# Projections of a group's last head placed 9, 14 and 9 pieces past the unit's last, where it was 5

## What is computed

```
for i in range(2):
    h = rmsnorm(x, pre_norm[i])
    proj = h @ w_in                     # 1024 x 3088 (GLA), 1024 x 5152 (SSD)
    # GLA: q, k, v, gate r, low-rank decay;  SSD: z, (x, B, C) through a conv of 4 taps, dt
    y = chunked_scan(proj) * silu(gate) # four heads or groups, a state carried from chunk to chunk
    y = rmsnorm_per_head(y) @ w_out
    x = x + rmsnorm(y, post_norm[i])
```

## Time and profile before

| | |
|---|---|
| median of 3 runs | 1531.34 us (1528.44 to 1532.91) |
| profiled execution | 1527.04 us |
| its span, first to last instruction | 1525.3 us |
| PE busy | 1422.1 us (93%) |
| DVE busy | 1170.3 us (77%) |
| ACT busy | 837.6 us (55%) |
| POOL busy | 241.8 us (16%) |
| mean granted TensorE clock | 0.982 of full |

### The profile page before, as it was taken

One profiled execution on the slowest core, in us unless ns is written; L12 is line 12 of the kernel. 1 busy time (PEld: TensorE's weight loads), 2 busy tenths in 40 slices (PEclk: granted clock), 3 DMA queues, 4 the chain that ended last, 5 costly groups with the idle time before them and its releaser, 6 DMA issues. The chain is left out here.

```text
span 1525.3 us, 31313 instructions
## 1 busy us (share of the span) xinstructions
PE 1422.1 (93%) x11554; PEld 1181.4 (77%) x11554; DVE 1170.3 (77%) x2592; ACT 837.6 (55%) x1877; POOL 241.8 (16%) x421
## 2 busy tenths in 40 slices
PE   6999998799999969999999999989999999999985
PEld 5989887667888759898888988867777777777754
DVE  4566687767777987968886998976879787687775
ACT  4745555365656545546565754654666474655451
POOL 5010122011422100011120220220012110000012
PEclk9999999999999989999999999999999999999998
DMA  7474556255576343458844855742675665555541
GB/s 201 129 222 127 184 174 219 79 170 166 156 200 191 105 129 96 139 125 222 250 119 134 275 149 157 226 128 78 195 226 150 179 180 151 173 153 156 174 139 62
DMA packets 284162, 247.34 MB, mean 162 GB/s; under 512 B 32696, under 2 KB 250908, under 8 KB 283340
## 3 DMA queue, kind: packets, MB, share of 16 engines
q1 hardware_dynamic: 274348, 212.51, 47.0%
q0 software_dynamic: 9664, 32.84, 7.9%
HBM read 184.59 MB, written 65.00 MB: 164 GB/s over the span
## 5 line engine op out<-in xcount | busy, mean ns | idle before, releaser
L1452 PE MATMUL bank<-h,w 128*128 128x268 f32 (+1 forms) x4752 | 834.7, 330 | 23.1 <-ACT w L863 16.2
L1452 PEld LDWEIGHTS bank<-h,w 128*128 128x128 f32 x4752 | 701.0, 191 | 100.9 <-issue 24.7
L879 DVE TENSOR_TENSOR w<-w_raw,w 128x1024 fp32r<-128x1024 f32 x132 | 160.9, 1219 | 38.0 <-ACT w L863 37.6
L848 PE MATMUL bank<-s_w_out,s_yt_hi 128*128 128x512 f32 (+2 forms) x544 | 169.8, 402 | 3.8 <-DVE s_ys L2546 3.8
L863 ACT ACTIVATE w<-w_raw 128x1024 fp32r<-128x1024 f32 x132 | 138.7, 1051 | 7.9 <-DMA w_raw<-in_ssd_w_in_dram 7.7
L1530 DVE SCALAR_TENSOR_TENSOR conv<-before_conv,cw,conv 128x260 f32<-128x260 f32 (+2 forms) x216 | 125.3, 580 | 4.2
L848 PEld LDWEIGHTS bank<-s_w_out,s_yt_hi 128*128 128x128 f32 (+2 forms) x544 | 97.0, 182 | 30.8 <-issue 4.4
L848 PE MATMUL bank<-g_w_out,g_ot_hi 128*128 128x512 f32 (+2 forms) x288 | 97.5, 427 | 1.5 <-DVE g_ot_lo L2088 1.3
L848 PE MATMUL bank<-s_w_out,s_yt_lo 128*128 128x512 f32 x240 | 95.6, 398 | 0.0
L2630 ACT ACTIVATE s_yt_hi<-bank 128x512 fp32r<-128x512 f32 (+1 forms) x36 | 20.1, 558 | 124.7 <-PE bank L2621 124.6
L2333 ACT ACTIVATE s_decay<-s_decay,t_ac 128x128 f32<-128x128 f32 (+1 forms) x288 | 85.5, 379 | 1.2
(11 more groups left out here) (258 smaller groups left out, 2465.5 us busy)
## 6 DMA issues: line engine op xcount, KB each, us to landing
w_raw<-in_ssd_w_in_dram SPq DMA_DIRECT2D x80, 512.0 KB, 4.3
w_raw<-in_gla_w_in_dram SPq DMA_DIRECT2D x48, 512.0 KB, 4.5
s_decay<-kept_acd SPq DMA_DIRECT2D x32, 512.0 KB, 6.4
w_raw<-in_ssd_w_out_dram SPq DMA_DIRECT2D x30, 512.0 KB, 4.0
g_chunk<-kept_gq SPq DMA_DIRECT2D x32, 448.0 KB, 5.1
s_chunk<-kept_sq SPq DMA_DIRECT2D x32, 384.0 KB, 4.8
kept_sq<-stage SPq DMA_DIRECT2D x80, 134.0 KB, 4.4
kept_sq<-stage SPq DMA_DIRECT2D x40, 256.0 KB, 4.9
```

The source lines that it names most:

```text
L848: last = pe.matmul(bank[0:r, :], yt[a][:, k, 0:r], wo[:, b, 512 * half:512 * half + 512], start=(k + a + b == 0), stop=(k == tiles - 1 and ...
L879: dve.tensor_tensor(self.part(i, 1), self.raw(i), hi, ALU.subtract).then_inc(self.w_lo, 1)
L1452: last = pe.matmul(bank[:, 0:n], w[:, p.tile % 2, a, k, :], h[:, b, k, c:c + n], start=(i == 0), stop=(i == len(terms) - 1))
```

## The change

`goal(k)` says up to which piece the order has gone when the mark of unit k is reached. It was five pieces past the last piece of that unit, for every unit. Now it is 9 past for units (0,0,3) and (1,0,3), 14 past for (0,1,3), and five for all others. No instruction is added or taken away. The pieces between the mark before and the mark behind each of these three units are placed anew among the scan's tasks, and with them all that hangs on pieces.

```
     def goal(self, k):
-        return self.spent((min(self.last[k] + 5, len(self.pieces)), 0))
+
+        L, G, u = UNITS[k]
+        ahead = {(0, 0): 9, (0, 1): 14, (1, 0): 9}.get((L, G), 5) if u == U - 1 else 5
+        return self.spent((min(self.last[k] + ahead, len(self.pieces)), 0))
```

## The result

The changed kernel takes 1541.43 us (median of 4 runs, 1539.89 to 1547.36), the kernel before, measured with it, 1532.12: ratio 1.0087, 95% interval 1.0066 to 1.0108 (the two medians alone give 1.0061). Measured again later beside other kernels it gave 1.0080 (1.0067 to 1.0094), 1539.77 us for 1527.91. The forecast was 1525.7 and faster; the range ended at 1538. The profiled execution took 1547.36 us, span 1545.6, that is 20.3 us more than before.

The account below looks back on a forecast made before the run. TensorE, 93% busy, was taken to bound the kernel, so only its waits and half clock could move. The middle of -10.1 and -3.8, -7.0, plus 1.4 for thinner filler gave -5.6 us: 1525.7 us, range 1517 to 1538.

Parts of the forecast that it names:

- Account A, saved: Pace estimate: steps leaving take their VectorE work along, saving 15.4 us at place 2 and 4.9 at place 1.
- starved stretch: Stretch up to a group's first projection, with norms as filler; PE idles, and VectorE was said to set the pace.
- place 2: Stretch up to low piece 118 (layer 0 group 1 unit's mark), 13.37 us idle of 62.30; 1.64 steps were to leave.
- place 1: Stretch up to low piece 79 (layer 0 group 0 unit's mark), 13.07 us idle of 80.10; 0.49 steps were to leave.
- Account A, the gain of a moved step: VectorE time saved less PE work given back: -6.2 us at place 2, -2.2 at place 1; -10.1 over all three.
- Account B, low pieces: Wait-by-wait estimate: waits before low pieces 79, 118 and 210 become 5.7, 6.9 and about 3.0 us; account's sum -3.8.
- Dense stretches: Stretches behind the low pieces: no cost behind places 1 and 3, 1.4 us for thinner conv filler behind place 2.
- place 3: Stretch up to low piece 210 (layer 1 group 0 unit's mark), 12.75 us idle of 127.00; some 0.45 steps leave.
- The clock: Half-clock stretches: two instead of three at place 2, -1.7 us; one of two goes in half the cases at place 1, -0.9.
- Slower by the low piece: Rival, chance 0.14: chains before low pieces 79 and 118 each 6 us longer, +6.4 us, 1538; decided past 18 us.
- Half clock under norms: Rival, chance 0.03: norm transposes at places 1 and 2 run at half clock, +11 us, 1543.
- Pace unchanged: Rival, chance 0.33: vanished waits return before the next attention or product matmul, conv stretch costs 4 us; +0.2, 1531.5.

Follow-up runs that it names:

- 8 and 10 pieces: Marks at 8, 10 and 6 pieces past the last instead of the changed kernel's 9, 14 and 9; ratio 1.0004 against the kernel before.
- 15 and 7: Marks at 5, 15 and 7 pieces instead of the changed kernel's 9, 14 and 9; 1522.94 us, ratio 0.9965 against the kernel before.
- the norms early: Changed kernel with copy and subtraction of a group's last two norms issued right behind the last norm piece; ratio 1.0043 against the kernel before.
- the early norms in the kernel before: Kernel before, with copy and subtraction of each group's last two norms issued right behind the last norm piece; ratio 0.9995.

## Why the prediction was wrong, step by step

- **What bounds the kernel.** Right that only waits and clock could move, and that PE's and DVE's work would stay. "PE's busy sum is unchanged" was wrong by 10.3 us, since busy time counts the clock.
- **Account A, saved.** The starved stretch of place 2 shortened by 15.3 us, for 15.4 worked out; place 1 by 4.5 for 4.9. Both hits are luck. The 15.4 was to be 9.2 of PE's work and 6.2 of idle time; it was 14.72 of PE busy and 0.55 of idle time.
- **Account A, the gain of a moved step.** This is the step that failed first: the idle time of the starved stretch was to leave along with the steps, and it stayed, 13.52, 12.82 and 12.33 us for 13.07, 13.37 and 12.75. Nothing then is left of -6.2. The work given back was also sized too small, 9.2 us at place 2 and 2.7 at place 1, by the share of a step in the planner's room. Between the old and the new position of piece 118 lie two sets of output products, two states, two attention products, two turns of v, and one each of keys, levels and turn: 5.6 us for a full step and 4.4 for the rest (446.29 to 452.13 less six matmuls of 0.24), 10.0 us at full clock. For piece 79 it is that rest alone, 4.4. What remains of the 14.72 is for the most part half clock: one set of output products takes 2.99 us at full clock and 4.15 in the starved stretch of before, where the clock is at half from 540.80 to 544.20:

```profile
448.79:451.78 2.99, 2.99 (x15) 2.37 (x14) 2.57 (x4) 0.69 (x1) 0.00 (x0) 1.00 0.93 278
541.47:545.62 4.15, 4.15 (x13) 3.26 (x14) 4.08 (x8) 0.00 (x0) 0.00 (x0) 0.67 0.86 304
```

  In the changed kernel the half clock of that stretch lies on the wait before the low piece, and the conv stretch behind it grew by 14.0 us: these 10.0, 1.4 of idle time, and 2.6 of busy time in which half clock has a part.
- **Account B, low pieces.** Foreseen 5.7, 6.9 and 3.0; measured 5.29, 8.40 and 3.20. The chain was right, and two weights cost 1.5 more. The wait of 3.44 at the attention product went, as did 3.75 and 1.39, which were to stay; waits of 1.48 and 2.28 us before norms and the longer low wait took their place. In sum idle 12.82 for 13.37.
- **Dense stretches.** "Behind places 1 and 3 DVE has room, so nothing": wrong at both, and the argument was of the wrong kind. A busy share of 65 or 77% says nothing of what stands ahead of one instruction. At place 1 the gate work of head piece 85 came behind the sample step of the scan, which itself waits for ScalarE 4.22 us; at place 3 the size sums came ahead of the turned outputs. The conv stretch was foreseen at 131 us with under 7 idle, and has 134.5 with 6.20; the 1.4 us counted for its thinner filler came true as idle time (1.36).
- **The clock.** The largest miss. One to one and a half half-clock stretches were to go; instead their time rose from 55 to 105 us. The sum treated a wait as its own length. In this kernel a wait of 3 to 8 us can take PE to half clock for 3.4 to 10.2 us, part of it over the work behind; that made half of the loss in the profile. It isn't a fixed price: the two low waits of 6 us with 8 and 10 pieces came with 67 us of half clock, and at place 1 with no loss.
- **The rivals.** "Slower by the low piece" had the right sign and a wrong condition: the two waits reached 5.3 + 8.4 = 13.7 us, short of 18, and the kernel was slower all the same; place 2, where the longer one is, costs nothing alone. "Half clock under norms" was rightly put low: the clock fell around waits, and transposes held it. "Pace unchanged" describes place 2: the waits came back elsewhere, idle 12.82 us for 13.37, and the place alone measured 0.9999. No rival had a wait at a head piece or at the transposes behind place 3, which are in the dense stretches.
- **The range** ended at 1538 because the one slower rival that it took in was a sum of two long waits; the costs at places 1 and 3, some 7 us each, were in no case of it.

Shown by runs: that each place acts alone; that place 1's cost is made up for when the last subtraction no longer queues behind the scan's work; that idle time brings the half clock, and filling it wins 3.4 us; that 15 and 7 together are better than 14 and 9. Argued from traces only: that the order of the size sums makes the wait at the `z_first` transposes, and how the two waits at place 1 work together. Its leg grows only where there are both: with 9 pieces (5.29 us at the low piece and 3.71 behind a head piece, 400 to 404) and with 7 (5.14 and 5.64, 398.2). With 8 there is only a long low wait (6.01, 395.1), with 9 and the norms early only the one behind the head piece (3.71, 395.0).

One thing more is in the table: the leg between places 2 and 3 is 202.1 to 202.5 us with place 3 at 5, and 203.2 or more in every kernel with another number there, though the order of the tasks is the same up to the end of that leg. With place 3 alone at 9 the clock accounts for it (idle 7.6 us for 7.8, busy 197.2 for 194.3). These are the same 18 matmuls in the kernel before and in that one:

```profile
733.31 2.49 PE L1452 MATMUL bank<-h,w 128*128 128x268 f32 x18 [2.14 <-DVE stage L1519]
...
734.11 4.39 PE L1455 MATMUL bank<-h,w 128*128 128x268 f32 x18 [2.14 <-DVE stage L1522]
```

The wait ahead is the same 2.14 us; in the second the clock is at 0.50 from 733.40 to 740.20. Why the half clock falls there is open.

## What to carry to other kernels

When filler is moved in a hand-made order, count the instructions that pass from one side to the other, on every engine; a share of planned room isn't that count. A starved stretch that gets shorter has gained only if its idle time falls. When an edit is to test a cause, look first whether it moves anything at the place that is meant; the early norms in the kernel before didn't. Look at the clock behind a wait as well as at its length: where a wait can't be avoided, work that computes nothing in it can pay. Then try the neighbours of a setting: 7 and 8, and 14 and 15, differ here by more than 5 and 9 do in the forecast.

## What the hardware showed

Idle times of 3.2 to 8.4 us were followed or accompanied by 3.4, 6.8 or 10.2 us at 1.2 GHz; in the profile of the kernel before it was 3.4 at a time in the starved stretches. That isn't fixed by the order: with only place 1 changed, place 2 is as before and its half clock is 6.8 us twice (545.50 to 552.30 and 559.10 to 565.90, both 0.50). The same wait of 2.14 us came with 6.8 us of half clock in one kernel and with none in another. Fp32 transposes of 128x128, 30 and 50 of them in two waits, kept the granted clock at 1.00. Two profiles of the same changed kernel show 105 and 89 us of half clock with the same order of work, a difference of 6.4 us in span (1545.6 and 1539.2): a single profile of this kernel doesn't settle a cost of that size.
